# First expert blocks loaded during the mixer, a router for all tokens at once, 8 KB runs, and a modulation turned in three groups

## What is computed

```python
c_act = silu(c)
mod = c_act @ w_ada + b_ada               # 6 vectors of 1024
sh1, sc1, ga1, sh2, sc2, ga2 = split(mod, 6)
u = modulate(rmsnorm(h, g_norm1), sh1, sc1)
h = h + ga1 * hybrid_mixer(u, ...)        # q, k, gt, a, r, v, gates; a gated scan; gla_o; w_out
u2 = modulate(rmsnorm(h, g_norm2), sh2, sc2)
lg = u2 @ w_rg + b_rg                     # 4 groups: the best one is taken
le = (u2 @ w_re + b_re)[best group]       # 8 experts in it: the two best
for e in range(32):                       # 32 experts, 1024 -> 512 -> 1024
    y += comb[:, e] * ((silu(u2 @ w1[e]) * (u2 @ w3[e])) @ w2[e])
h = h + ga2 * y
h = modulate(rmsnorm(h, g_final), *split(c_act @ w_ada_f + b_ada_f, 2))
```

## Time and profile before

| what | value |
|---|---|
| median of 3 runs | 1499.39 us (1494.62 to 1499.64) |
| the profiled execution | 1498.59 us |
| its span, first to last instruction | 1496.8 us |
| mean granted TensorE clock | 0.900 |
| TensorE busy / weight loads | 1241.3 us (83%) / 963.9 us (64%) |
| VectorE / ScalarE busy | 675.6 us (45%) / 456.6 us (31%) |
| moved by DMA | 374.51 MB, mean 250 GB/s |

### The profile page before, as it was taken

One profiled execution on the slowest core, in us unless ns is written; L12 is line 12 of the kernel. 1 busy time (PEld: TensorE's weight loads), 2 busy tenths in 40 slices (PEclk: granted clock), 3 DMA queues, 4 the chain that ended last, 5 costly groups with the idle time before them and its releaser, 6 DMA issues.

```text
span 1496.8 us, 20521 instructions
## 1 busy us (share of the span) xinstructions
PE 1241.3 (83%) x8742; PEld 963.9 (64%) x8742; DVE 675.6 (45%) x1139; ACT 456.6 (31%) x652; POOL 1.9 (0%) x15
## 2 busy tenths in 40 slices
PE   6989989996966566565766679999999989899998
PEld 3679888894412122121321169999998879899986
DVE  2546987544100000000000065366557777577974
ACT  1533344533000000000000053343435545445453
POOL 0000000000000000000000000000000000000000
PEclk8999989996878887886877789999999999999999
DMA  9886632869999999999999857443454424445552
GB/s 339 280 274 213 219 112 88 282 222 360 399 387 399 393 393 399 387 399 390 395 396 389 332 184 218 127 141 113 127 157 153 140 86 163 134 161 178 197 197 85
DMA packets 226569, 374.51 MB, mean 250 GB/s; under 512 B 8855, under 2 KB 121897, under 8 KB 226345
## 3 DMA queue, kind: packets, MB, share of 16 engines
q1 hardware_dynamic: 226304, 369.58, 69.7%
q0 software_dynamic: 144, 3.54, 0.7%
q10 hardware_dynamic: 24, 0.03, 0.0%
HBM read 372.03 MB, written 4.62 MB: 252 GB/s over the span
## 4 chain that ended last, share of the span: by engine, by line
PE 52%; SPq 23%; DVE 11%; DMA 8%; ACT 3%; issue 3%; DVEq 0%; ACTq 0%
PE bank L554 30%; SPq L2473 23%; DMA arena<-in_w 4%; PE bank L1133 4%; DVE arena L1164 4%; DVE fine L1156 3%; DMA above<-in_w 2%; DVE arena L1156 2%; ACT fine L1912 2%; PE bank L827 2%; PE bank L551 2%; PE bank L604 2%; ACT arena L1912 1%; PE bank L582 1%; DMA arena<-in_w_in 1%
## 5 line engine op out<-in xcount | busy, mean ns | idle before, releaser
L554 PE MATMUL bank<-fine 128*128 128x256 f32 x4656 | 584.4, 288 | 28.6 <-DVE fine L1156 18.0
L554 PEld LDWEIGHTS bank<-fine 128*128 128x128 f32 x4656 | 573.9, 195 | 38.0 <-issue 35.2
L1156 DVE TENSOR_TENSOR fine<-arena,fine 128x1024 fp32r<-128x1024 f32 (+2 forms) x263 | 300.3, 1167 | 175.7 <-ACT fine L1912 166.1
L1912 ACT ACTIVATE fine<-arena 128x1024 fp32r<-128x1024 f32 (+2 forms) x279 | 267.1, 984 | 175.3 <-PE bank L554 97.6
L1912 ACT ACTIVATE arena<-bank 128x256 f32<-128x256 f32 (+2 forms) x161 | 73.6, 483 | 592.6 <-PE bank L838 194.6
L827 PE MATMUL bank<-arena 128*32 128x512 f32 x640 | 106.4, 803 | 75.5 <-DMA arena<-in_w 75.5
L1156 DVE TENSOR_TENSOR arena<-arena,bank 128x512 f32<-128x512 f32 x8 | 5.5, 688 | 299.8 <-PE bank L827 299.7
L827 PEld LDWEIGHTS bank<-arena 128*32 128x32 f32 x640 | 20.6, 129 | 155.0 <-DMA arena<-in_w 103.1
L1912 ACT ACTIVATE arena<-arena 128x512 f32<-128x512 f32 (+6 forms) x95 | 63.5, 697 | 157.6 <-DVE arena L1156 67.6
L1164 DVE SCALAR_TENSOR_TENSOR arena<-arena 128x256 f32<-128x256 f32 (+2 forms) x265 | 108.2, 474 | 1.2 <-ACT arena L1912 0.8
L827 PE MATMUL bank<-above,arena 128*32 128x512 f32 x384 | 61.7, 778 | 39.4 <-DMA above<-in_w 39.4
(11 more groups left out here) (160 smaller groups left out, 807.3 us busy)
## 6 DMA issues: line engine op xcount, KB each, us to landing
arena<-in_w SPq DMA_DIRECT2D x240, 512.0 KB, 11.7
above<-in_w SPq DMA_DIRECT2D x144, 512.0 KB, 11.4
arena<-in_w_in SPq DMA_DIRECT2D x62, 1024.0 KB, 5.4
arena<-in_w_ada SPq DMA_DIRECT2D x24, 1024.0 KB, 8.7
arena<-in_ffn_w_up SPq DMA_DIRECT2D x22, 1024.0 KB, 5.1
arena<-in_ffn_w_down SPq DMA_DIRECT2D x11, 1024.0 KB, 4.9
arena<-in_w_ada_f SPq DMA_DIRECT2D x8, 1024.0 KB, 12.3
arena<-in_w_gla_o SPq DMA_DIRECT2D x4, 1024.0 KB, 9.0
```

What stands on the lines that cost most here:

```text
L554: ins = e.matmul(o, w[:, k, j * P:j * P + P], x[:, kt, :], start=start, stop=stop, skip_group_check=True)
L1156: return e.tensor_tensor(o, a, b, f)
L1912: return e.activation(o, i, f, bias=bias, scale=scale)
```

## The change

1. **Modulation.** The 16 rows form three groups (0 to 3, 4 to 9, 10 to 15). All rows of a group are summed into one PSUM bank, row i of the group on partition i of each 32, by a weight window of cz, in which the activated c stands in column 5 of 37 and the rest is 0. So a group needs one copy and one turn. The first 8 chunks have a slot each and wait for nothing. Row 8 moves forward into level 0 of the scan, row 9 into level 1, rows 10 and 11 into level 2. Chunk f from 11 to 23 still waits for the products of chunk f - 3. Rows 12 to 15 remain in the last part, chunks 24 and 25 now wait for o_made, chunk 26 for act_on["conv"].
2. **First piece.** For u1, u2 and u3, make_first makes the products with the high part of x for all 8 tiles first, then those with the low part. Around q the high and low halves are interleaved with the tiles of u.
3. **Early blocks.** The 8 slots are laid anew; three of them lie where scr, zp, St, qb and others lay in the mixer. Blocks 0 to 2 are issued among the loads of gla_o, after on_turned[1, 1] (block 1 also after lnorm_v["scaled"]). Block 3 waits for the low half of the last w_out piece, blocks 4 to 6 for its products, block 7 for u. Block n from 8 on waits for the products of the pair that block n - 8 is in.
4. **8 KB runs.** w1, w3 and w2 are laid as (p t): a partition gets 8 (or 4) rows that follow each other. A block holds two experts instead of four, half of their rows, as two DMAs of 1 MB with one run of 8 KB for each partition. Two blocks are needed for the matmuls of either. uT and hid are written in the order that goes with it.
5. **Router.** The logits are made as 36 rows of 256 tokens (8 matmuls, each as soon as its tile of u is there), the bias is added, and two matmuls turn them. All 256 tokens are routed by one set of instructions. The one-hot matrix is made for the first quad alone first; the rest of it, the weights (comb) and the overflow flag come behind the first gather.

```diff
+        early_at = ARENA - 3 * WIDE
+        early = [arena[:, at:at + WIDE] for at in (early_at + WIDE, early_at + 2 * WIDE, early_at)]
+        wides = early + [arena[:, 0:WIDE]] + [above[:, WIDE * i:WIDE * i + WIDE] for i in range(FINE // WIDE)] + [
+            arena[:, WIDE:2 * WIDE]]
-        w1v, w3v, w2v = (T[n][0].rearrange("(j e) (t p) n -> j p e t n", e=4, p=P) for n in ("w1", "w3", "w2"))
+        w1v, w3v, w2v = (T[n][0].rearrange("(j e) (p t) n -> j p e t n", e=4, p=P) for n in ("w1", "w3", "w2"))
...
             if f < 8:
-                return f % 4, ada_slots[f % 4], f - 4 if f >= 4 else None
+                return f, ada_slots[f], None
+        ADA = (range(0, 4), range(4, 10), range(10, 16))
...
+                for kt in range(4 * half, 4 * half + 4):
+                    e.wait_ge(*x_hi_a[name, "tile", kt])
+                    products(kt, x_hi, True, start=kt == 0)
+                if half:
+                    for kt in range(KT):
+                        e.wait_ge(*x_lo_v[name, "tile", kt])
+                        ins = products(kt, x_lo, False, stop=kt == KT - 1)
...
-                        ins = e.matmul(bank[32 * k:32 * k + 32, :], cact[:, kt:kt + 1].to_broadcast([P, 32]), slot[:, k, :],
-                                       start=f % 2 == 0, stop=f % 2 == 1, skip_group_check=True)
+                        ins = e.matmul(banks[7][32 * k:32 * k + 32, :], cz[:, kt, 5 - i:37 - i], slot[:, k, :],
+                                       start=f == 2 * ADA[g][0], stop=f == 2 * ADA[g][-1] + 1, skip_group_check=True)
...
-                    ada_sums(7 + li)
-                if li < 4:
-                    ada_to_mod(6 + li)
+                    ada_sums((7, 9, 10)[li])
+                if li == 0:
+                    ada_sums(8)
+                if li == 2:
+                    ada_sums(11)
+                    ada_to_mod(1)
...
+            bank = misc(route, "columns")
+            for k in range(KT):
+                e.wait_ge(*(scaled_a if k % 2 else scaled_v)[1, k])
+                ins = e.matmul(bank[0:36, 0:256], wr[:, k, :], u[:, k, :], start=k == 0, stop=k == KT - 1)
+            ins.then_inc(*router.up("columns"))
...
+                    for th in range(2):
+                        slots = []
+                        for pair in range(2):
+                            s, slot, n = wide_of(quad, 4 * wn + 2 * th + pair)
+                            e.wait_ge(*wide_in[s][n])
+                            slots.append(slot)
...
+            def expert(quad, i):
+                s, slot, n = wide_of(quad, i)
+                if n >= NW:
+                    prior, pi = (n - NW) // 12, (n - NW) % 12
+                    e.wait_ge(*(up_made[prior, pi | 1] if pi < 8 else down_made[prior, pi - 8 | 1]))
+                elif n < len(early):
+                    e.wait_ge(*on_turned[1, 1])
...
+                for x in range(2):
+                    e.dma_start(slot[:, x, :, :], src[quad, :, 2 * (i % 2) + x, at:at + kt, :]).then_inc(*wide_in[s].up(n, 16))
...
-            load("gla_o", 2)
-            ada(11)
-            load("gla_o", 2)
-            ada(12)
+            load("gla_o", 1)
+            expert(0, 0)
+            load("gla_o", 1)
+            expert(0, 1)
+            ada(13)
+            load("gla_o", 1)
+            expert(0, 2)
+            load("gla_o", 1)
+            ada(14)
             load("w_out", 2)
-            ada(13)
+            ada(15)
             load("w_out", 2)
-            ada(14)
-            ada(15)
```

More of the change, by code:

```diff
@@ L432, in build @@
         out_written = [signal(f"out_written{i}") for i in range(4)]
-        ada_in = [signal(f"ada_in{i}") for i in range(4)]
+        ada_in = [signal(f"ada_in{i}") for i in range(8)]
         ring_in = [signal(f"ring_in{i}") for i in range(NS)]
@@ L527, in misc, with make_first, products @@
                 return take(b, done, label)
+            def make_first(p, half, bank):
+                name, ph = FACTOR[p.name], int(p.n >= PIECES1)
+                def products(kt, x, both, start=False, stop=False):
+                    parts = [shaped(w[:, 0:4 * p.width], 4, p.width) for w in w_parts[ph][(2 * p.n + kt // 4) % NU]]
+                    for j in range(p.width // P):
+                        for i, w in enumerate(parts[:1 + both]):
+                            ins = e.matmul(bank[:, j * 256:j * 256 + 256], w[:, kt % 4, j * P:j * P + P], x[ph][:, kt, :],
+                                           start=start and i + j == 0, stop=stop, skip_group_check=True)
+                    return ins
+                for kt in range(4 * half, 4 * half + 4):
[5 more added lines that the diff above has]
+                        ins = products(kt, x_lo, False, stop=kt == KT - 1)
+                        if kt % 4 == 3:
+                            ins.then_inc(*products_of.up((p.n, kt // 4)))
             def make(half_at):
@@ L539, in make @@
                 first = p.i == 0 and FIRST[FACTOR[p.name]] == p.name
-                if first and FACTOR[p.name] not in TILE_BY_TILE:
+                if first and FACTOR[p.name] in TILE_BY_TILE:
+                    make_first(p, half, bank)
+                    return
+                if first:
                     e.wait_ge(*x_lo_v[FACTOR[p.name], half])
@@ L775, in tensor_program @@
+            turn_u(0, 0)
             bank = misc(route, "logits")
-            e.wait_ge(*scaled_v[1, 6])
-            e.wait_ge(*scaled_a[1, 7])
+            e.wait_ge(*route["columns"])
             for tc in range(2):
-                for k in range(KT):
-                    ins = e.matmul(bank[:, 36 * tc:36 * tc + 36], u[:, k, tc * P:tc * P + P], wr[:, k, :], start=k == 0,
-                                   stop=k == KT - 1)
+                ins = e.matmul(bank[:, 36 * tc:36 * tc + 36], lgc[0:36, tc * P:tc * P + P], ident[0:36, 0:36], start=True, stop=True)
@@ L782, in tensor_program @@
             ins.then_inc(*router.up("logits"))
[L783 to L791 removed]
+            turn_u(0, 1)
@@ L792, in tensor_program @@
+            turn_u(1, 0)
+            turn_u(1, 1)
+            bank = take(1, route, "count")
+            e.wait_ge(*route["mask"])
             e.wait_ge(*consts_late[0])
@@ L1558, in vector_program @@
-            ins.then_inc(*route.up("hot"))
+            logits = shaped(bank_of(route, "logits")[:, 0:72], 2, 36)
+            l4, le = logits[:, :, 0:4], logits[:, :, 4:36]
+            step(e.reduce_max(gm[:, :, 0], l4, AX))
+            tt(ex, l4, over(gm, 4), ALU.subtract).then_inc(*route.up("ex"))
+            step(tt(oh4, l4, over(gm, 4), ALU.is_equal))
+            step(tt(t4, oh4, repeat(down4, 2), ALU.mult))
+            step(e.reduce_max(mx[:, :, 0], t4, AX))
+            step(tt(oh4, t4, over(mx, 4), ALU.is_equal))
@@ L1560, in gather_tokens, with hot_of @@
+            ranks = bank_of(route, "count")
+            step(stt(slotn, shaped(ranks[:, 0:64], 2, 32), 1.0, mask, ALU.add, ALU.mult))
+            def hot_of(e0, n):
+                at = iota[:, 1:CAP + 1].rearrange("p (o x c) -> p o x c", o=1, x=1).to_broadcast([P, 2, n, CAP])
+                return tt(hot[:, :, e0:e0 + n, :], over(slotn[:, :, e0:e0 + n], n, CAP), at, ALU.is_equal)
+            hot_of(0, 4).then_inc(*route.up(("hot", 0)))
             def gather_tokens(quad):
@@ L2479, in sync_program @@
                     e.reg_load(reg, idxb[0:1, 16:17])
-                for i in range(12):
+                for i in range(0 if quad else len(early), 12):
                     expert(quad, i)
```

453 lines of the change are left out of this document (225 added, 228 removed).

## The result

| | before | after |
|---|---|---|
| median of 5 runs | 1499.39 us | 1485.78 us |
| lowest to highest | 1494.62 to 1500.2 | 1481.87 to 1487.0 |
| profiled execution, span | 1498.6 us, 1496.8 us | 1485.78 us, 1484.0 us |

The ratio is 0.9904, 95% interval [0.9892, 0.9916]: faster by 14 us, where the forecast was 47 and the range began at 29. The sign was right and the size was not. Two places of the trace show why.

What follows compares the result with a forecast made beforehand. The prediction took the expert loads' rate and starting moment to set the end, with TensorE and VectorE alternating as bound in the mixer. 1498.6 - 31 - 14 - 4 + 3.5 - 1.5 = 1451.6, median 1452 us; range 1434 to 1470.

Steps and rivals of the forecast that it cites:

- Term 1: Loads of the 88 later expert blocks: 8 KB runs bring 5.03 us a block in place of 5.38, -31 us.
- The first and third rivals: Expert loads: nothing gained beyond 4 KB, 1465 us, chance 0.17; nothing gained by the runs at all, 1483 us, chance 0.08.
- the slower layout: Expert loads: neighbouring partitions reading 16 KB apart are served badly, all 88 blocks pay, +40, 1523 us; chance 0.06.
- Term 2: From w_out through the router: block 8's first bytes come at 368.4 in place of 382.9, -14 us.
- The cover that I named for gla_o: Mixer's last part: gla_o's weights up to 5.4 us late, but TensorE stays three halves behind the splitting, 10 us.
- The bound of +5: Mixer's last part: without cover, early blocks make weights late at w_out, up to +5 us; the forecast took 0.
- The second rival: Before block 8: late weights or a slow chain let it start no sooner, 1466 us; chance 0.09.
- Term 3: Start and mixer: earlier q and fewer turns, less waits for rows 8 and 11, -4 us, bounds -9 and +3.
- Term 4: Tail and first pieces: 32 records behind the last landing where 16 stood, +3.5 us; u2 and u3 high part first, -1.5.
- the first pieces: At u2 and u3: starting from the high part wins about one tile each, -1.5 us (0 to -3).
- the 370 us: First expert matmul: expected near 359; the forecast is wrong if it comes after 370.

Runs made afterwards that it cites:

- experiment 5: Experts' blocks read with the old row order (2 KB runs of w1 and w3, 4 KB of w2), on the changed kernel: 1511.85 us, ratio 1.0098.
- experiment 4: Blocks 0 to 2 of the experts issued behind the last piece of w_out, not among gla_o's, on the changed kernel: 1479.27 us, ratio 0.9879.
- trace of 7: Row 11's sums behind the scores of level 3 and blocks 0 to 2 issued behind w_out, on the changed kernel: 1459.8 us, ratio 0.9745.
- Experiment 1: GpSimd spreads the bias rows after the router's transposes, not after level 2's scores, on the changed kernel: 1472.31 us, ratio 0.9824.
- experiment 3: TensorE's sums of row 11 moved behind the scores of level 3, not level 2, on the changed kernel: 1461.52 us, ratio 0.9750.
- experiment 2: GpSimd spreads the bias rows two levels sooner, after level 0's scores, on the changed kernel: 1484.32 us, ratio 0.9906.
- the last three experiments: On the changed kernel, row 11's sums behind level 3's scores, plus row 8 later, or no early blocks, or both with late bias spreading: 1461.5, 1459.8, 1458.59 us.

## Why the prediction was wrong

**Term 1, the rate: right.** -31 forecast, 26 to 30 measured (experiment 5), 4.99 us a block against 5.03. The first and third rivals are out, and so is the slower layout: partitions 16 KB apart are read at 420 GB/s. The rule of the Trainium skill's page "DMA: Bandwidth & Descriptors" (Specifications) that memory gives a core about 358 GB/s does not hold here, and the measurement decides. The Trainium skill's page "Perfetto Trace Analysis" (Roofline) says that on trn2 a core that alone is active can go above that share and is bounded by its 16 DMA engines at some 435 GB/s; with 420 GB/s at a DMA share of 1.01 to 1.02 this case agrees.

**Term 2, block 8: right behind norm(1), wrong ahead of it.** 28.9 us from norm(1) to the first expert product, 30.3 forecast (24.4 to 28.9 in the traces of the experiments); the loads stand still for 13 us, 11 forecast; the head start itself is worth nothing, as argued. What failed is "The early loads go into gaps ... So 0". The gap at 332 us that I named exists, but the three blocks are not issued there: they go out between 284 and 308 us, among the loads of gla_o and row 13, and from 298 to 310 us the loads run at 414 and 381 GB/s. The cover that I named for gla_o held. What I put at nothing without a look were the chunks of row 13 behind blocks 0 and 1, which TensorE needs as they land. The bound of +5 was the better number (4 us by experiment 4, 5.8 by the trace of 7). The second rival named late weights in this part; but it had block 8 gain nothing, and the router's gain stood.

**Term 3, the mixer: this is the step that failed.** "At level 2 row 11 waits likewise, but there VectorE is the bound; I give +1." Measured: +20.8 us in that level. Experiment 1 splits them: 8.2 remain without GpSimd's transfer, where I had +1, and 12.6 are that transfer's, which I had not counted at all.
- *The cover.* VectorE is full there, 16.00 of 16.00 us, but TensorE is too, 15.87 (the window of the kernel before, above). A second engine that is full gives no cover to the first. Experiment 1 shows it: with a wait of only 3.2 us level 2 still takes 8.2 us longer, and the lower clock after the wait, which has no term in the prediction, is part of that.
- *The landing time.* I took 5.4 us, the median of w_in's loads. For a chunk alone that was right: row 8's second chunk landed in 5.2 us (104.53 to 109.70), and row 11's in 5.1 in experiment 1. The page of the kernel before has a longer median for w_ada, but chunks issued in pairs are in it, as at 130 us with 7.7 and 8.0 us:

```profile
arena<-in_w_ada SPq DMA_DIRECT2D x24, 1024.0 KB, 8.7
```

- *The neighbour.* GpSimd's transfer stood in the trace of before, in the window in which the new chunk would travel (DMA view of 150 to 180 us):

```profile
scratch<-scratch POOLq DMA_DIRECT2D x1, 3456.0 KB, 14.4
```

I counted what the moved step passes on SP, and not what GpSimd sends at that moment. That trace could not show what the transfer does to a load, for none was issued in its first 12 us. But it named the risk: if the chunk ends no sooner than the transfer, 14.4 us, of which the first half of the row covers 1 to 2, the wait is an estimated 13 us. That belonged in the range.

The start was as forecast (first q product 35.97, in place of 39.87; level 0 at 98.87, in place of 105.50), and level 0 took it all back (level 1 at 129.61, before 129.63):

```profile
105.50 3.78 PE L679 MATMUL bank<-arena 128*128 128x128 f32 x16 [4.90 <-DVE arena L1156]
...
129.63 1.95 PE L679 MATMUL bank<-arena 128*128 128x128 f32 x16
```

Row 8's sums and its 3.57 us wait make level 0 6.6 us longer (+3 and +1.9 forecast). That the start came out so well is in part luck of the execution: in the nine traces of kernels that are alike up to there, level 0 starts between 98.85 and 104.54 us (last section).

Another 2.5 us were lost where nothing was touched: from level 3 to the pointwise products it takes 99.35 us in place of 96.85, and the scores of level 6, in that stretch, take 3.46 us in place of 2.05, a sign of the lower clock. The stall does not explain it: experiment 3, without a stall, has 99.88 and 3.70 us, experiment 2, with the stall in level 0, 96.72 and 2.05. The cause stays open.

**Term 4: right in size.** From the last landing (839.99) to the first product of the last sum over experts 6.9 us, before 2.7 (the earlier trace rows and the next line of that view, 859.02): +4.2, forecast +3.5. From there to the end it is 637.1 us in place of 637.8: the first pieces brought 0.7 of 1.5.

**The sum.** Norm(1) came at 362.65; forecast was 329 (339.32 - 4 - 6.3). These 33.6 us are the whole miss of 34 (1485.8 against 1451.6): 19.8 in level 2 (20.8 against +1), 6.5 from the pointwise products on, 3.9 up to level 2 (-0.9 in place of -6 - 3.7 + 1.9 + 3), 2.5 from level 3 to the pointwise products, 0.9 in rounding and in the 0.7 us that the forecast gave to the root behind norm(1). The first expert product came at 391.51, past the 370 us that I had named as the sign of a wrong forecast. Every step behind norm(1) came out within 2 us. The range was too narrow on the slow side for the same reason: the bound of term 3 was +3, and neither a wait without cover (8.2 us in experiment 1) nor the transfer (12.6) was in it.

## What to carry to other kernels

A load can be late by what shares the DMA engines with it, on any queue: before a step is put behind a load, list all transfers in that window, GpSimd's among them, and take the landing time of a load in the same company, not a median. Look also at what a new load puts back in its own queue: here it was row 13, not the weights that I had checked. An engine that is bound beside another full engine hides nothing; look up the slack of the engine that will wait. A step that waits is best put behind work that is ready: one level later the same late chunk cost a wait of 0.83 us.

## What was not expected of the hardware

**A transfer from memory to memory on GpSimd's queue holds up a load beside it.** 3.54 MB go in 144 packets, 24.6 KB each, beside 3.14 MB in 2111 packets of 1.5 KB, and the load ends 2.5 us after the big transfer instead of sharing with it evenly (2.2 and 2.3 us after it in experiments 2 and 3). The Trainium skill's page "DMA: Bandwidth & Descriptors" (Queues, rings and completion order) says that each DMA engine takes turns between its queues packet by packet; by that rule 9 large packets an engine (144 / 16) would go by in the first 9 turns of the small ones, and the load would end shortly after the transfer, which is what the rows show. That takes the packets of the profile for those of the page, and no run here changed their size, so this cause is only argued.

**The clock of the start differs between executions of almost the same program.** In 36 to 44 us, with the same busy time, the changed kernel and the kernel of experiment 3 (untouched up to there):

```profile
36.00:44.00 8.00, 8.00 (x41) 6.27 (x42) 7.46 (x17) 6.15 (x11) 0.00 (x0) 0.79 1.07 369
```

```profile
36.00:44.00 8.00, 8.00 (x24) 4.47 (x25) 7.46 (x17) 6.17 (x10) 0.00 (x0) 0.50 1.08 369
```

The rise from 1.2 to 2.4 GHz comes later (in 44 to 52 us the clock is 1.00 in the one, 0.70 in the other), and level 0 starts at 104.54 in place of 98.87. In the nine traces of kernels that are alike up to there, it starts at 98.85 to 99.38 in five, at 102.50 and 102.54 in two, and at 104.21 and 104.54 in two. Such 5.7 us are more than the differences between the last three experiments; how much of the spread between runs they make is not shown, since each kernel has one trace.
